# The block inverse of the gated delta rule on two 64x64 diagonal tiles in place of four 32x32 tiles

## The reference

```python
def gated_delta_rule(q, k, v, g, beta):
    # Recurrence: S_t = a_t (S_{t-1} - beta_t k_t k_t^T S_{t-1}) + beta_t k_t v_t^T,  o_t = S_t^T q_t
    kb, vb = k * beta, v * beta
    decay = exp(where(causal, g[..., :, None] - g[..., None, :], NEG_INF))
    lower = where(strict, einsum('bhncd,bhnmd->bhncm', kb, k) * decay, 0.0)
    t_inv = triangular_solve(lower + eye, eye, left_side=True, lower=True, unit_diagonal=True)
    u = t_inv @ vb
    w = t_inv @ (kb * exp(g)[..., None])
    a_intra = where(causal, einsum('bhncd,bhnmd->bhncm', q, k) * decay, 0.0)
    def step(s, xs):
        v_new = uc - einsum('bhcd,bhde->bhce', wc, s)
        o = einsum('bhcd,bhde->bhce', qd, s) + einsum('bhcm,bhme->bhce', ac, v_new)
        s = s * exp(gl)[..., None, None] + einsum('bhcd,bhce->bhde', kt, v_new)
```

## Time and profile before

| | us |
|---|---|
| median of 3 runs (lowest, highest) | 2332.67 (2330.41, 2332.84) |
| the profiled execution | 2336.52 |
| its span, first to last instruction | 2334.7 |
| PE busy | 2154.0 (92%) |
| DVE busy | 1418.4 (61%) |
| ACT busy | 1017.3 (44%) |
| mean granted clock of TensorE | 0.942 |

### The profile page before, as it was taken

One profiled execution on the slowest core, in us unless ns is written; L12 is line 12 of the kernel. 1 busy time (PEld: TensorE's weight loads), 2 busy tenths in 40 slices (PEclk: granted clock), 3 DMA queues, 4 the chain that ended last, 5 costly groups with the idle time before them and its releaser, 6 DMA issues.

```text
span 2334.7 us, 41043 instructions
## 1 busy us (share of the span) xinstructions
PE 2154.0 (92%) x18458; PEld 1955.0 (84%) x18458; DVE 1418.4 (61%) x1598; ACT 1017.3 (44%) x1063; POOL 135.9 (6%) x79
## 2 busy tenths in 40 slices
PE   6789999889999999898967999999998998699998
PEld 6778988769988998896757799899888876588996
DVE  8866655566655555867743665465468486357554
ACT  5564443544443443453632444344344537134442
POOL 1000000000001000400000020020021001002000
PEclk9799999989999999999966999999999999589999
DMA  7144555415555654653310465556546433014753
GB/s 187 18 149 145 184 186 181 134 37 163 181 189 188 191 182 154 198 182 107 126 38 2 144 210 188 177 177 201 177 160 204 151 109 126 4 55 147 219 186 117
DMA packets 259288, 342.90 MB, mean 147 GB/s; under 512 B 23112, under 2 KB 169198, under 8 KB 259112
## 3 DMA queue, kind: packets, MB, share of 16 engines
q1 hardware_dynamic: 253968, 329.95, 44.1%
q0 software_dynamic: 2544, 9.08, 1.3%
q10 hardware_dynamic: 2599, 1.23, 0.4%
HBM read 338.14 MB, written 2.10 MB: 146 GB/s over the span
## 4 chain that ended last, share of the span: by engine, by line
PE 78%; DVE 10%; ACT 6%; issue 4%; DMA 2%; ACTq 0%; POOL 0%; DVEq 0%; POOLq 0%
PE acc L1704 20%; PE acc L1706 20%; PE acc L1705 20%; DVE w_lo L1080 3%; PE acc L1720 3%; PE trp L2168 3%; ACT w_hi L636 2%; PE acc L1727 2%; PE acc L2163 1%; DMA raw<-in_w_in 1%; PE acc L1769 1%; PE trp L1704 1%; PE acc L2147 1%; PE trp L1706 1%; PE trp L1705 1%
## 5 line engine op out<-in xcount | busy, mean ns | idle before, releaser
L1080 DVE TENSOR_TENSOR w_lo<-raw,w_hi 128x2048 fp32r<-128x2048 f32 (+1 forms) x316 | 737.0, 2335 | 515.1 <-ACT w_hi L636 514.5
L636 ACT ACTIVATE w_hi<-raw 128x2048 fp32r<-128x2048 f32 (+1 forms) x316 | 593.6, 1879 | 643.2 <-PE acc L1706 287.6
L1704 PE MATMUL acc<-xT_hi,w_hi 128*128 128x256 f32 x2496 | 710.3, 285 | 14.7 <-DVE w_lo L1080 14.7
L1705 PE MATMUL acc<-xT_lo,w_hi 128*128 128x256 f32 x2496 | 709.6, 284 | 0.0
L1706 PE MATMUL acc<-xT_hi,w_lo 128*128 128x256 f32 x2496 | 709.4, 284 | 0.0
L1704 PEld LDWEIGHTS acc<-xT_hi,w_hi 128*128 128x128 f32 x2496 | 482.7, 193 | 15.6 <-issue 15.4
L1705 PEld LDWEIGHTS acc<-xT_lo,w_hi 128*128 128x128 f32 x2496 | 482.7, 193 | 0.0
L1706 PEld LDWEIGHTS acc<-xT_hi,w_lo 128*128 128x128 f32 x2496 | 482.6, 193 | 0.0
L1705 PE MATMUL acc<-w_lo,hT_hi 128*128 128x512 f32 x528 | 208.6, 395 | 0.0
L1706 PE MATMUL acc<-w_hi,hT_lo 128*128 128x512 f32 x528 | 208.6, 395 | 0.0
L1704 PE MATMUL acc<-w_hi,hT_hi 128*128 128x512 f32 x528 | 208.6, 395 | 0.0
(11 more groups left out here) (370 smaller groups left out, 2818.7 us busy)
## 6 DMA issues: line engine op xcount, KB each, us to landing
raw<-in_ffn_w SPq DMA_DIRECT2D x184, 512.0 KB
raw<-in_w_in SPq DMA_DIRECT2D x60, 1024.0 KB
raw<-in_ffn_w_up SPq DMA_DIRECT2D x88, 512.0 KB
raw<-in_ffn_w SPq DMA_DIRECT2D x40, 1024.0 KB
raw<-in_ffn_w_down SPq DMA_DIRECT2D x20, 1024.0 KB
raw<-in_ssm_w_glu SPq DMA_DIRECT2D x16, 512.0 KB
raw<-in_kv_w SPq DMA_DIRECT2D x8, 1024.0 KB
raw<-in_w_branch_a SPq DMA_DIRECT2D x8, 1024.0 KB
```

Of the source, the lines that this page charges most:

```text
L636: A(w_hi[:, p % SPL, 0:kt, :], raw[:, p % RAW, 0:kt, :], ACT.Copy).then_inc(hi_ready, 1)
L1080: V_.tensor_tensor(w_lo[:, p % SPL, 0:kt, :], raw[:, p % RAW, 0:kt, :], w_hi[:, p % SPL, 0:kt, :].bitcast(F32), ALU.subtract).then_inc(lo_ ...
L1704: mm(out, ah, bh, start=first, stop=False, skip_group_check=True)
L1705: mm(out, ah, bl, start=False, stop=False, skip_group_check=True)
```

## The change

The block size `BL` goes from 32 to 64 and the number of levels `SMALL` from 5 to 6. Each level now works on the two 64x64 diagonal blocks of a head, `side(0)` and `side(1)`. There are 2x8x2 products for Y and 2x2x8x2 for Z in a level, 96 in all, of 64x64x64; the sixth level leaves out the transpose for one block. One step of 64x64 products then joins the two blocks to 128. `T64`, `Y64`, `X4` and `wide_bank` are gone. `UT`, `Ys` and `Lc` are twice as wide; the masks are made for two levels at a time (`masked`), the first pair before the inverse, the second after the first level, the third in the middle of the fourth. Z goes to the `acc` buffers, each half of `U` is placed by ScalarE, and `rows(nat..v)` with its reading on VectorE is moved ahead of `kk` and `qk`, because `Lc` and `Ys` lie over the values. GpSimd clears one quarter of `U` instead of `U` and `T64`.

```diff
-SMALL = 5
-BL = 32
+SMALL = 6
+BL = 64
...
-        UT = Ti_flat[:, 0:1024].rearrange("p (t s h m) -> p t s h m", t=TT, s=2, m=BL)
-        Lc = UT[:, :, 1]
-        T64 = Ti_flat[0:64, 1024:2048].rearrange("p (t h m) -> p t h m", t=TT, m=64)
-        Xs = Xm_flat.rearrange("p (t v h m) -> p t v h m", t=TT, v=4, m=BL)
+        UT = Ti_flat.rearrange("p (t s h m) -> p t s h m", t=TT, s=2, m=BL)
+        Ys = Yp_flat[:, 0:1024].rearrange("p (t h m) -> p t h m", t=TT, m=BL)
+        Lc = Yp_flat[:, 1024:2048].rearrange("p (t h m) -> p t h m", t=TT, m=BL)
...
-            uses(f"nat{i}k", 2), uses(f"kk{i}", 2), uses(f"qk{i}", 2), uses(f"nat{i}v", 2)
+            uses(f"nat{i}k", 2), uses(f"nat{i}v", 2), uses(f"kk{i}", 2), uses(f"qk{i}", 2)
+            for lv in range(1, SMALL + 1):
+                for t in range(TT):
+                    uses(f"Z{i}_{lv}_{t}", 1)
...
+                for t in range(TT):
+                    pool.wait_ge(sem(f"Y_filled{t}"), 7 * i + 2)
+                pool.wait_ge(sem("sz_ready"), i + 1)
+                nc.gpsimd.memset(U[side(1), :, :, side(0)].rearrange("p t h m -> p (t h) m"), 0.0).then_inc(sem("U_cleared"), 1)
...
+                    for b in range(2):
+                        A(Lc[side(b), t], L[side(b), t, :, side(b)], ACT.Copy).then_inc(sem(f"L_blocks{t}"), 1)
+                for lv in range(1, SMALL):
                     for t in range(TT):
                         act.wait_ge(sem(f"Y_filled{t}"), 7 * i + lv + 1)
-                        A(Ys[:, t], small_bank(trp[t])[:, 0], ACT.Copy).then_inc(sem(f"Y_copied{t}"), 1)
...
+                        A(Ys[:, t], small_bank(trp[t]), ACT.Copy).then_inc(sem(f"Y_copied{t}"), 1)
...
+                for t in range(TT):
+                    scaled_rows(use[f"nat{i}v"] + t, vb[:, t], sm[:, 0, t])
                 decayed("kk", L)
                 decayed("qk", AT)
...
+                def masked(t, two):
+                    levels = const(C_LVL + 2 * two * BL, 2 * BL).rearrange("p (v m) -> p v m", m=BL)
+                    V_.tensor_tensor(Xs[two][:, t], bc(Lc[:, t], 1, 2), bc(levels, 2, DH), ALU.mult).then_inc(sem(f"X_ready{t}"), 1)
...
                 for lv in range(1, SMALL):
                     for t in range(TT):
-                        dve.wait_ge(sem(f"Z_filled{t}"), 6 * i + lv)
-                        V_.tensor_tensor(UT[:, t], UT[:, t], small_bank(trp[2 + t]), ALU.subtract).then_inc(sem(f"UT_ready{t}"), 1)
...
+                        u = use[f"Z{i}_{lv}_{t}"]
+                        wait_filled(dve, u)
+                        if lv == SMALL - 1:
+                            step(V_.tensor_tensor(UT[side(1), t, 0], UT[side(1), t, 0], Z2(u)[side(1), 0], ALU.subtract))
+                            step(V_.tensor_tensor(UT[side(0), t], UT[side(0), t], Z2(u)[side(0)], ALU.subtract))
+                            step.settle()
+                            dve.sem_inc(*freed(u))
+                        else:
+                            V_.tensor_tensor(UT[:, t], UT[:, t], Z2(u), ALU.subtract).then_inc(*freed(u))
+                        if lv == 3:
+                            dve.wait_ge(sem(f"Y_filled{t}"), 7 * i + 4)
+                            masked(t, 2)
+                for t in range(TT):
+                    u = use[f"Z{i}_{SMALL}_{t}"]
+                    wait_filled(dve, u)
+                    step(V_.tensor_scalar(U[side(0), t, :, side(1)], Z2(u)[side(0), 0], -1.0, None, ALU.mult))
+                    step.settle()
+                    dve.sem_inc(sem(f"U_ready{t}"), 1)
+                    dve.sem_inc(*freed(u))
...
                 rows(use[f"nat{i}k"], kh)
+                rows(use[f"nat{i}v"], vh)
                 with_keys(use[f"kk{i}"], kh)
                 pe.wait_ge(sem("qk_normed"), 4 * i + 4)
                 with_keys(use[f"qk{i}"], qh)
-                rows(use[f"nat{i}v"], vh)
...
+                for lv in range(SMALL):
+                    for t in range(TT):
+                        pe.wait_ge(sem(f"X_ready{t}"), 3 * i + lv // 2 + 1)
+                        if lv == 1:
+                            pe.wait_ge(sem(f"U_started{t}"), i + 1)
+                        elif lv > 1:
+                            wait_evacuated(pe, use[f"Z{i}_{lv - 1}_{t}"])
+                        for h in range(DH):
+                            for b in range(2):
+                                q = side(b)
+                                ins = tile(small_bank(trp[t])[q, h], Xs[lv // 2][q, t, lv % 2, h, :], UT[q, t, 0, h, :] if lv else ident[q, q])
+                        ins.then_inc(sem(f"Y_filled{t}"), 1)
+                    if lv == 0:
+                        continue
+                    for t in range(TT):
+                        u = use[f"Z{i}_{lv}_{t}"]
+                        claim(u)
+                        pe.wait_ge(sem(f"Y_copied{t}"), SMALL * i + lv)
+                        for h in range(DH):
+                            for b in range(2):
+                                q = side(b)
+                                tile(Z2(u)[q, 0, h], UT[q, t, 1, h, :], Ys[q, t, h, :])
+                        for h in range(DH):
+                            for b in range(2 if lv < SMALL - 1 else 1):
+                                q = side(b)
+                                ins = tile(Z2(u)[q, 1, h], Ys[q, t, h, :], UT[q, t, 1, h, :])
+                        ins.then_inc(acc_ready, 1)
```

More of the change, by code:

```diff
@@ L432, in small_bank, with Z2, side @@
         def small_bank(bank):
[L434 to L442, removed]
+            return bank[:, :].rearrange("p (h m) -> p h m", m=BL)
+        def Z2(u):
+            return acc[u % 2][:, :].rearrange("p (s h m) -> p s h m", s=2, m=BL)
+        def side(b):
+            return slice(BL * b, BL * b + BL)
         def bc(ap, axis, n):
@@ L1593, in _ @@
                 scaled_rows(use[f"nat{i}k"] + 1, kbg[:, :, :], sm[:, 6, 1])
+                for t in range(TT):
+                    scaled_rows(use[f"nat{i}v"] + t, vb[:, t], sm[:, 0, t])
                 decayed("kk", L)
                 decayed("qk", AT)
+                def masked(t, two):
+                    levels = const(C_LVL + 2 * two * BL, 2 * BL).rearrange("p (v m) -> p v m", m=BL)
+                    V_.tensor_tensor(Xs[two][:, t], bc(Lc[:, t], 1, 2), bc(levels, 2, DH), ALU.mult).then_inc(sem(f"X_ready{t}"), 1)
                 for t in range(TT):
[L1597 to L1599 removed]
+                    dve.wait_ge(sem(f"L_blocks{t}"), 2 * (i + 1))
+                    masked(t, 0)
                 for t in range(TT):
[L1601 to L1606, removed]
+                    dve.wait_ge(sem(f"X_ready{t}"), 3 * i + 1)
+                    step(V_.tensor_tensor(UT[:, t, 1], bc(const(C_SID, BL), 1, DH), Xs[0][:, t, 0], ALU.subtract))
                 step.settle()
@@ L2198, in _ @@
-                for t in range(TT):
-                    pe.wait_ge(sem(f"UT_ready{t}"), SMALL * (i + 1))
-                    for h in range(DH):
-                        for b in (0, 2):
-                            ins = tile(small_bank(trp[t])[quadrant(b), 0, h], L[quadrant(b + 1), t, h, quadrant(b)], UT[quadrant(b + 1), t, 0, h, :])
+                        ins = tile(small_bank(trp[t])[side(0), h], L[side(1), t, h, side(0)], UT[side(1), t, 0, h, :])
                     ins.then_inc(sem(f"Y_filled{t}"), 1)
@@ L2204, in _ @@
                 for t in range(TT):
-                    pe.wait_ge(sem(f"Y_copied{t}"), 6 * i + SMALL)
+                    u = use[f"Z{i}_{SMALL}_{t}"]
+                    claim(u)
+                    pe.wait_ge(sem(f"Y_copied{t}"), SMALL * (i + 1))
                     for h in range(DH):
-                        for b in (0, 2):
-                            tile(small_bank(trp[2 + t])[quadrant(b), 0, h], UT[quadrant(b), t, 1, h, :], Ys[quadrant(b), t, h, :])
-                        ins = tile(small_bank(trp[2 + t])[quadrant(1), 1, h], Ys[quadrant(0), t, h, :], UT[quadrant(0), t, 1, h, :])
@@ L2210, in _ @@
-                    ins.then_inc(sem(f"Z_filled{t}"), 1)
+                        ins = tile(Z2(u)[side(0), 0, h], UT[side(0), t, 1, h, :], Ys[side(0), t, h, :])
+                    ins.then_inc(acc_ready, 1)
+                pe.wait_ge(sem("U_cleared"), i + 1)
                 for t in range(TT):
-                    pe.wait_ge(sem(f"U_ready{t}"), 7 * i + 6)
-                    for h in range(DH):
-                        ins = tile(wide_bank(trp[t])[:, h], L[64:P, t, h, 0:64], U[64:P, t, h, 64:P])
@@ L2215, in _ @@
-                    ins.then_inc(sem(f"Y_filled{t}"), 1)
-                for t in range(TT):
-                    pe.wait_ge(sem(f"T64_ready{t}"), 3 * (i + 1))
-                    pe.wait_ge(sem(f"Y_copied{t}"), 6 * (i + 1))
-                    for h in range(DH):
-                        ins = tile(wide_bank(trp[2 + t])[:, h], T64[:, t, h, :], Y64[:, t, h, :])
-                    ins.then_inc(sem(f"Z_filled{t}"), 1)
-                for t in range(TT):
```

(2 more changed lines are left out.)

64 lines of the change are left out of this document (10 added, 54 removed).

## The result

The change makes the kernel faster: 2304.07 us (median of 4 runs, 2301.37 to 2304.97) against 2332.76 (4 runs, 2330.41 to 2337.56). The ratio is 0.9872, with a 95% interval of 0.9855 to 0.989: 28.7 us less. Forecast were 2341 in a range of 2330 to 2354, so the sign and the range are both wrong. It is the first rival, a clock of 1.00 in the inverse, that came true, between its two numbers (2284, or 2308 if the clock comes up halfway).

The account below looks back on a forecast made before the run. Delivery of TensorE's instructions was taken to bound the inverse. At half clock, 60.6 us per inverse against 56.83 and 54.71, less 0.6 each, gave +8.5 us: 2345.0 profiled, 2341 for the median, range 2330 to 2354.

Parts of the forecast that it names:

- the first rival: Inverse in both mixers: clock at 1.00, 48 us less in all, 2284, or 2308 if it rises halfway; chance 0.14.
- What bounds the kernel now: Inverse before the change: TensorE waits for its own instructions, 3.92 us per round of 128 records, 3.75 in second mixer.
- Records and their cost at 0.50: Inverse: 992 records after the first step instead of 1760, each 53.3 ns on two tiles at half clock.
- The head: Before the first doubling: values turned earlier, two masks gone, so the inverse's start comes 0.6 us sooner in each mixer.
- The clock: Inverse in both mixers: clock stays at 0.50 from about 1197 to the heads, making each inverse 60.6 us.
- the "against" of the first rival: Clock in the inverse: one busy 64*64 tile stayed at 0.50 for 6.72 us; it rose only after 5.74 us of 128*128 records.
- The Trainium skill on the clock: Clock in the inverse: depends on how busy TensorE is, whatever part of the array works; by it the first rival wins.
- The rule of the Trainium skill: Both 64*64 tiles write one PSUM bank: records would go one by one, 48 us more per mixer, 2437; chance 0.03.
- The first rival's own number: Inverse at full clock: 27.8 us for instructions, 3.4 + 2.5 for the last step, 1.0 for masks, 34.7 us together.
- the terms that I had called covered at 0.50: Levels 1 to 4: copies of Y and subtractions of Z hide behind the other chunk's 1.7 or 3.4 us on TensorE.
- level 5 with the last step: End of the inverse at half clock: 6.8 + 3.4 us, then 6.8 us for 64 records plus 0.6 of waiting.
- The heads: After the inverse: slow start of 5.74 and 4.45 us at 0.50 unchanged; bounds 2.9 us less or 1 us more each.

Follow-up runs that it names:

- the clock alone: Kernel before plus one unused wide product after each chunk's Y and Z in the four 32x32 levels: 2331.13 us against 2330.39.
- the last kernel: Changed kernel with the last pair's masks moved ahead of the third level's subtractions and each level's subtraction cut in two: 2288.86 us against 2330.39 before.
- the kernel with the subtraction in two: Changed kernel with each level's subtraction cut in halves, the half the next Y reads first and signalled separately: 2295.95 us against 2330.39 before.
- the kernel with one block: Changed kernel with only the first 64x64 diagonal block multiplied in the first step and all levels: 2340.21 us against 2330.39 before.
- filler bursts: Kernel before plus four unused wide products after the Y and four after the Z of each 32x32 level: 2351.74 us against 2328.33.

## Why the prediction was wrong, point by point

- **What bounds the kernel now: right.** A round of 128 small records cost 3.5 to 3.9 us, with 1.9 us of work in it or 2.6, at either clock. Three tiles for four took the inverse from 56.83 to 42.38 us, about in proportion to the records, and the clock alone gave 0.2 and 1.2 us.
- **Records and their cost at 0.50: right.** 992 records, and while the clock was at 0.50 they came at 54 ns for a forecast 53.3. Held at 0.50 by one block, the inverse took 60.57 us for 60.6.
- **The head: right in sign, a little small.** 1.1 and 0.7 us less for a forecast 0.6. In the second mixer VectorE's start of `UT` is last, as forecast; in the first it is TensorE's own first step (3.01 us from 1188.39), which the sum did not look at.
- **The clock: wrong, and the whole miss.** Each inverse was forecast at 60.6 us and took 41.5 and 41.7, in all 38.0 less, and the forecast of 2341 was 37 too high. The step that failed is the "against" of the first rival: one 64\*64 tile kept the clock at 0.50 with 6.72 of 6.72 us busy, two were put "between these two" (that and the 128\*128 records of the heads), and I took the lower side, with 0.14 for the other. That was a guess at the one quantity which decided the sign: there was no row for two tiles at once over any length of time, and 6.72 us of one tile said only what one tile does. The runs show that the reading of one tile was right (0.50 for 59.55 and for 86.79 us without a stop) and that with two it rose (to 1.00, after 3.36 us of work in 3.41) and stayed up for 34.13 us. With the evidence there was, the two sides deserved about equal chances, and the range should have reached down to the rival's 2284.
- **The Trainium skill on the clock** (TensorE: Matmul & The Clock Gate, The HAM clock gate) makes it depend on how busy the engine is. For two tiles it forecast the result; for one tile the measurements speak against it. By these runs it cannot be used by itself where a product fills only a part of the array. The rule of the Trainium skill, TensorEngine Tiling, Gotcha 1: PSUM Pressure, that row tiles cannot use one PSUM bank at the same time, is not borne out: two tiles wrote one bank at 29 ns a record.
- **The first rival's own number: too low.** It had 34.7 us for an inverse at full clock; measured 41.5 and 41.7. A level was put at 5.76, the instruction rate, and took 6.29, since the subtraction is no longer covered once Y takes half the time: the terms that I had called covered at 0.50 were not looked at again at 1.00. That is 0.5 for each of two levels; the one with the masks took 2.1 more than 5.76 (7.85), for a forecast 1.0; the first level began at half clock (7.90 - 5.76 = 2.1); and level 5 with the last step, partly at half clock, took 13.2 for 4.8 + 5.9. Together 1.1 + 1.1 + 2.1 + 2.5 = 6.8, which is the miss. With the cover restored the last kernel has 35.31 and 35.18.
- **The heads: half right.** I took no change in their slow start; it went from 5.74 to 4.24 us and from 4.45 to 4.5 (the clock rose at 2022.3, 4.5 after the start). The 2.9 us that the bounds and the first rival had for full clock in the heads are about right: 14.53 us for 17.27 in the kernel with the subtraction in two.

Size of the parts at the end: fewer and larger products at half clock would have cost 4 to 6 us in each mixer (by the kernel with one block), the clock without them gave at most 1.2, and both together gave 15.3 and 13.0. The change takes a limit away that the clock doesn't touch, the delivery, and puts one in its place that the clock halves, so neither part shows its worth alone.

## What to carry to other kernels

Where a kernel has very many small products, count instructions first: here 256 of TensorE's instructions took 3.5 to 3.9 us to arrive, at either clock, and only a kernel with fewer of them could use a faster clock. When a forecast turns on a clock of 0.50 or 1.00, work out the times for both and let the range hold both, unless a row shows that very use of the array (how many tiles at once, for how long without a stop) at one of them. And when an engine gets twice as fast, go through its handovers again: let the half of an evacuation that the next product reads come first, and put work that nobody waits for where the evacuating engine is idle.

## What the runs showed of the hardware

- The granted clock did not follow TensorE's busy time alone; what part of the array worked, or how many records passed, counted too (the two are not told apart): one 64\*64 tile for 86.79 us, 98% busy, at 0.50; two such tiles for 34.13 us, 88% busy, at 1.00; four tiles of 32\*32 with stops, 53% busy, at 0.50, and the same with a few 128\*512 products among them, 80% busy, at 1.00. Whether four 32\*32 tiles without stops would bring the clock up is open: it wasn't tried.
- Stops for instructions are as long at full clock with filler bursts (1.90 to 2.36 us) as at half without (1.5 to 2.1).
- Two 64\*64 tiles side by side: 54 ns a record at 0.50, 29 at 1.00, a little more than half. One tile after another does not cost the sum of both: 88 ns a record for 107, with the first records of the next tile beside the last three of the one before.
